# mLSTM's gate rows spread by DMA instead of by products, and HGRN2's first head with its filling products laid out anew

## What is computed

```
D[t, s] = exp(A_s - M_t) for s <= t, else 0
out_t   = sum_s D[t, s] (q_t . k_s) v_s / max(|sum_s D[t, s] (q_t . k_s)|, exp(-m_t))
```

## Time and profile before

| | |
|---|---|
| median of 3 runs | 1817.59 us (1816.62 to 1820.44) |
| the profiled execution | 1817.66 us, span 1815.8 us |
| mean granted clock of PE | 0.987 |
| PE | 1736.1 us busy, 96% |
| DVE, ACT, POOL | 1089.1 us (60%), 851.8 us (47%), 429.7 us (24%) |
| mLSTM | about 38 to 156 us of the span |
| HGRN2's first head | about 801 to 841 us |

### The profile page before, as it was taken

The page is one execution under the profiler, slowest core; times in us unless marked ns, Lnnn a source line. Parts: engine busy times, 40 slices in busy tenths (PEclk is TensorE's granted clock), DMA queues, the critical chain, the costliest instruction groups (busy, mean ns, idle before and its releaser), DMA issues. The chain is left out here.

```text
span 1815.8 us, 23867 instructions
## 1 busy us (share of the span) xinstructions
PE 1736.1 (96%) x8346; PEld 1396.6 (77%) x8346; DVE 1089.1 (60%) x1705; ACT 851.8 (47%) x1450; POOL 429.7 (24%) x332
## 2 busy tenths in 40 slices
PE   7998998999999999988999998999999989999997
PEld 5676887877888888777888887888888866677775
DVE  5545454458666643478878858765653377687343
ACT  5563555445333333456656645433332354255563
POOL 0332554110111100115554630111110013132232
PEclk9999999999999999999999999999999999999999
DMA  5111110231322232312112212222223222121121
GB/s 200 47 70 58 47 36 22 77 111 58 103 94 92 80 117 92 104 58 71 56 61 70 70 47 92 83 96 100 92 93 99 97 70 73 48 85 54 47 70 47
DMA packets 39904, 140.28 MB, mean 77 GB/s; under 512 B 4496, under 2 KB 4752, under 8 KB 39696
## 3 DMA queue, kind: packets, MB, share of 16 engines
q1 hardware_dynamic: 39824, 139.23, 22.6%
HBM read 137.11 MB, written 2.10 MB: 77 GB/s over the span
## 5 line engine op out<-in xcount | busy, mean ns | idle before, releaser
L187 PE MATMUL bank<-u_high,w_high 128*128 128x512 f32 x1580 | 649.8, 411 | 16.1 <-DVE m_on L1928 3.3
L189 PE MATMUL bank<-u_high,w_low 128*128 128x512 f32 x1580 | 621.0, 393 | 0.0
L188 PE MATMUL bank<-u_low,w_high 128*128 128x512 f32 x1580 | 620.7, 393 | 0.0
L187 PEld LDWEIGHTS bank<-u_high,w_high 128*128 128x128 f32 x1580 | 300.2, 190 | 102.5 <-issue 38.8
L189 PEld LDWEIGHTS bank<-u_high,w_low 128*128 128x128 f32 x1580 | 299.3, 189 | 65.8
L151 ACT ACTIVATE w_high<-w_ring 128x1024 fp32r<-128x1024 f32 x233 | 244.1, 1052 | 225.1 <-PE bank L189 173.1
L188 PEld LDWEIGHTS bank<-u_low,w_high 128*128 128x128 f32 x1580 | 300.5, 190 | 58.4 <-issue 3.8
L160 DVE TENSOR_TENSOR w_low<-w_ring,w_high 128x1024 fp32r<-128x1024 f32 x176 | 221.1, 1259 | 179.4 <-ACT w_high L151 179.2
L160 POOL TENSOR_TENSOR w_low<-w_ring,w_high 128x1024 fp32r<-128x1024 f32 x57 | 136.0, 2395 | 521.9 <-ACT w_high L151 521.8
L881 ACT ACTIVATE conv_up<-bank,col_sb 128x512 f32<-128x512 f32 x88 | 68.6, 780 | 270.5 <-DVE bank L936 270.5
L996 POOL TENSOR_TENSOR hidden<-conv_up 128x512 f32 x44 | 58.2, 1324 | 493.9 <-DVE conv_up L947 373.7
(11 more groups left out here) (413 smaller groups left out, 2316.5 us busy)
## 6 DMA issues: line engine op xcount, KB each, us to landing
w_ring<-ffn_up SPq DMA_DIRECT2D x88, 512.0 KB, 3.4
w_ring<-ffn_down SPq DMA_DIRECT2D x44, 512.0 KB, 3.4
w_ring<-c_in SPq DMA_DIRECT2D x32, 512.0 KB, 3.4
w_ring<-g_in SPq DMA_DIRECT2D x16, 512.0 KB, 4.2
w_ring<-m_in SPq DMA_DIRECT2D x12, 512.0 KB, 5.1
w_ring<-fox_in SPq DMA_DIRECT2D x12, 512.0 KB, 3.5
w_ring<-dsa_in SPq DMA_DIRECT2D x12, 512.0 KB, 3.5
w_ring<-ab_out SPq DMA_DIRECT2D x8, 512.0 KB, 4.4
```

Of the source, the lines that this page charges most:

```text
L187: nc.tensor.matmul(out, a[0], b[0], start=start, stop=False)
L188: nc.tensor.matmul(out, a[0], b[1], start=False, stop=False)
L189: return nc.tensor.matmul(out, a[1], b[0], start=False, stop=stop)
```

## The change

It has two parts.

In mLSTM: the eleven spreads by PE other than that of head 0's M are removed, with DVE's copies of them. In their place SP writes r_M, r_G and r_b (4 x 512 each, 8 KB) to a scratch in DRAM (`row_scratch`), waits for the writes to land, and reads them back with a source that repeats over the 128 partitions: M of heads 1 to 3 into a new tile `bcms`, G and b of four heads into `k.bcg`. These issues stand behind the loads of head 2's tiles and ahead of those of head 3's. DVE's arguments wait for `m_in`. PE's scores no longer wait for `spread_used`; those of head 1 wait for `cols_ready`, DVE's copy out of bank b4. The small columns are made at the end of DVE's head 1 instead of head 0, after a wait for `gb_in`; ACT's exponentials move from head 1 to head 2, DVE's last product from head 2 to head 3. PE's filling units are the same and keep their order; the two ahead of each spread join those that follow.

In HGRN2: the list for head 0 is [10, 12, 14, 16, 18, 20, 22, 24, 26, 27, 29, 32] instead of [16, 19, 20, 21, 22, 23, 24, 25, 26, 27, 28, 32], so ten units instead of sixteen stand ahead of the scores, and two instead of one behind each level. Head 1's f is projected into the output bank b_o instead of b_f, without the wait for head 0's f to be taken; the output of head 0 waits until DVE has taken it from there.

```diff
-    slots_first = [16, 19, 20, 21, 22, 23, 24, 25, 26, 27, 28, 32]
+    slots_first = [10, 12, 14, 16, 18, 20, 22, 24, 26, 27, 29, 32]
...
                     if m == 0:
                         k.wait_split(pe, 4 * h + s)
-                        pe.wait_ge((f_taken, q_taken, g_taken, v_ready)[s], h)
-                    ins = k.project(k.ps[s][:, :], s, None, m, m + 1)
+                        if h > 1 or s:
+                            pe.wait_ge((f_taken, q_taken, g_taken, v_ready)[s], h)
+                    ins = k.project((b_o if h == 1 and s == 0 else k.ps[s])[:, :], s, None, m, m + 1)
...
                 pe.wait_ge(at_done, 8 * h + 8)
+                if h == 0:
+                    pe.wait_ge(f_taken, 2)
...
-                nc.vector.tensor_tensor(out[:, :], k.ps[s][:, :], k.rn[:, :], ALU.mult).then_inc(done, 1)
+                bank = b_o if h == 1 and s == 0 else k.ps[s]
+                nc.vector.tensor_tensor(out[:, :], bank[:, :], k.rn[:, :], ALU.mult).then_inc(done, 1)
...
+    bcms = sb("m_M_next", [P, H - 1, T], F32)
+    rows = nc.dram_tensor("row_scratch", (3 * HA, T), F32).ap()
...
+            def spread_rows(out, kind, first, done):
+                n = HA - first
+                src = rows[kind * HA + first:(kind + 1) * HA, :].rearrange("(a h) t -> a h t", a=1).to_broadcast([P, n, T])
+                sp.dma_start(out, src).then_inc(done, 16)
+
             for h in range(2, H):
                 for s in range(3):
                     k.wait_split(sp, 3 * h - 3 + s)
                     k.load(sp, s, weights[3 * h + s, :, :])
+                if h == 2:
+                    sp.wait_ge(m_rows, 1)
+                    sp.dma_start(rows[0:HA, :], r_M).then_inc(rows_out, 16)
+                    sp.wait_ge(rows_out, 16)
+                    spread_rows(bcms[:, :, :], 0, 1, m_in)
+                    sp.wait_ge(g_rows, 1)
+                    sp.dma_start(rows[HA:2 * HA, :], r_G).then_inc(rows_out, 16)
+                    sp.wait_ge(b_ready, 1)
+                    sp.dma_start(rows[2 * HA:3 * HA, :], r_b).then_inc(rows_out, 16)
+                    sp.wait_ge(rows_out, 48)
+                    spread_rows(k.bcg[:, 0, :, :], 1, 0, gb_in)
+                    spread_rows(k.bcg[:, 1, :, :], 2, 0, gb_in)
...
                 pe.wait_ge(qk_ready, h + 1)
-                pe.wait_ge(bcm_ready, h + 1)
-                pe.wait_ge(spread_used, used[h])
+                if h == 0:
+                    pe.wait_ge(bcm_ready, 1)
+                if h == 1:
+                    pe.wait_ge(cols_ready, 1)
...
                 if n < H:
-                    pe.wait_ge(wt_ready, NT * h + NT)
-                    spread_row(b5, r_M, n).then_inc(m_spread, 1)
-                if n < H:
                     turn_v(n)
...
-                for i, (kind, g) in enumerate(spreads[h]):
-                    fill(2)
-                    if i == 0:
-                        pe.wait_ge(*((y_ready, h) if h else (cols_ready, 1)))
-                    elif i == 1:
-                        pe.wait_ge(bcm_ready, n + 1)
-                    else:
-                        pe.wait_ge(spread_used, used[h] + i - 1)
-                    spread_row(b_s[i % 2], (r_G, r_b)[kind], g).then_inc(spread, 1)
                 fill(len(units))
...
-                if h == 1:
+                if h == 2:
                     act.wait_ge(cols_done, 1)
...
-                dve.wait_ge(bcm_ready, h + 1)
+                dve.wait_ge(*((m_in, 16) if h else (bcm_ready, 1)))
+                m = bcms[:, h - 1, :] if h else bcm
...
-                for i, (kind, g) in enumerate(spreads[h]):
-                    dve.wait_ge(spread, used[h] + i + 1)
-                    nc.vector.tensor_copy(k.bcg[:, kind, g, :], b_s[i % 2][:, :]).then_inc(spread_used, 1)
-                if h == 0:
-                    dve.wait_ge(spread_used, H)
+                if h == 1:
+                    dve.wait_ge(gb_in, 32)
+                    dve.wait_ge(cols_ready, 1)
...
-                if h == 2:
+                if h == 3:
                     dve.wait_ge(cols_exp, 1)
```

More of the change, by code:

```diff
@@ L1510, in mlstm @@
     acc, vraw, on, bcm = (sb(f"m_{s}", [P, T], F32) for s in "acc v_raw on M".split())
+    bcms = sb("m_M_next", [P, H - 1, T], F32)
+    rows = nc.dram_tensor("row_scratch", (3 * HA, T), F32).ap()
+    (rows_out, m_in, gb_in) = (sem("row_" + s) for s in ("out", "m_in", "gb_in"))
     q, kk = (sb(f"m_{s}", [DK, T], F32) for s in "q k".split())
@@ L1522, in mlstm @@
     gb = lambda i: k.p("gbias", i)[0:HA]
-    (raw_taken, if_ready, tanh_done, f_soft, ab_taken, a_soft, b_ready, m_rows, g_rows, m_turned, m_cols, e_ready, g_turned, spread, spread_used,
+    (raw_taken, if_ready, tanh_done, f_soft, ab_taken, a_soft, b_ready, m_rows, g_rows, m_turned, m_cols, e_ready, g_turned,
      cols_ready, cols_exp, cols_done) = (sem("ab_" + s) for s in (
-         "raw_taken if_ready tanh_done f_soft ab_taken a_soft b_ready m_rows g_rows m_turned m_cols e_ready g_turned spread spread_used "
+         "raw_taken if_ready tanh_done f_soft ab_taken a_soft b_ready m_rows g_rows m_turned m_cols e_ready g_turned "
          "cols_ready cols_exp cols_done").split())
@@ L1530, in mlstm @@
          "d_masked st_done wt_ready num_done den_taken squared tot_ready on_scaled o_turned y_ready ch_act ch_dve ch_pool").split())
-    spreads = {0: [(0, h) for h in range(H)], 1: [(1, 0), (1, 1)], 2: [(1, 2), (1, 3)], 3: []}
-    used = {h: sum(len(spreads[g]) for g in range(h)) for h in range(H + 1)}
     def cs(c):
@@ L1904, in body @@
                 if n < H:
-                    take_m(n)
                     arguments(n)
@@ L1950, in _ @@
             dve.wait_ge(m_cols, 1)
-            take_m(0)
+            take_m()
             arguments(0)
```

8 lines of the change are left out of this document (4 added, 4 removed).

## The result

The changed kernel takes 1799.21 us, the median of 4 runs (1799.07 to 1801.34), against 1817.52 (1816.62 to 1820.44, 4 runs) for the kernel before beside it: a ratio of 0.9899, 95% interval 0.9882 to 0.9916, or 18.3 us. The forecast was 1797.6 with a range of 1794.0 to 1803.0.

What follows compares the result with a forecast made beforehand. PE was taken as the bound, busy 1736.1 of 1815.8 us. From 1817.66 us, 15.8 for mLSTM and 4.3 for HGRN2's first head were subtracted, giving 1797.6 us, with a range of 1794.0 to 1803.0.

Steps and rivals of the forecast that it cites:

- M spreads: mLSTM heads 1 to 3: removing three row spreads of M from PE saves 1.06 us each, 3.2 us.
- joint to head 3: mLSTM, end of head 2: last b spread and the 0.99 us wait for VectorE's copy go, 2.10 us.
- 1.7 us for the clock: mLSTM, after the gap before head 3's scores: work lost to the low clock, counted as won.
- The broadcasts: mLSTM, SP's queue: at some 400 GB/s M lands near 53, G and b near 64, cost 0.
- B: Rival: broadcasts slow at 82 GB/s, PE stands for head 3's tile, 7 us given back, 1804.6; chance 0.08.
- C: Rival: broadcasts delay head 3's loads over 20 us, PE stands after head 1's scores; one case 1819.6; chance 0.05.
- HGRN2's first head: HGRN2 head 0: earlier start and scores, fewer waits and steady clock win 4.4 us, taken as 4.3.
- VectorE's earlier work may slow GpSimd: HGRN2 head 0: GpSimd's factor pairs may lengthen beside VectorE's earlier work; 0.1 us taken off.
- moves with it: HGRN2 head 0: the chain to the turned keys follows level 4's merge, 3.4 us earlier, 834.07 becoming 830.65.
- 33.0 us is work: HGRN2 head 0, PE's start to head 1's scores: 39.5 us less 4.8 of waits and 1.7 of clock.
- The bank: HGRN2 head 0's start: projecting into the output bank lets PE start at 801.15 instead of 801.94, 0.8 us.
- A of the rivals: HGRN2's first head or head 3's joint: clock falls again, or waits return; 1799.3 to 1801.0; chance 0.17.

Runs made afterwards that it cites:

- m_one_engine: Changed kernel with M's broadcast issued in two parts, to 127 partitions and to the last one: 1806.89 us (one run).
- only_mlstm: Changed kernel with its three HGRN2 edits undone, leaving the mLSTM part alone: 1797.9 us, ratio 0.9903 to the kernel before.
- bank_only: Changed kernel with HGRN2's old list of products for head 0, keeping the new bank: 1799.33 us, ratio 0.9904 to the kernel before.
- late_queries: Changed kernel; HGRN2 head 0: split of head 1's fourth tile earlier, list ending 26, 28, 30, 32, GpSimd's decayed queries after all factors: 1799.33 us.
- pool_order: Changed kernel, with GpSimd making the factors of levels 4 and 5 before decayed keys and queries in HGRN2's head 0: 1800.73 us (one run).

## Why the prediction was right, and where it was not

- **mLSTM, 15.8 us forecast, 16.2 measured.** The price of a spread of G or b, 1.26 us with its joints, was 1.24. The M spreads, priced at 1.06, were worth 1.2 to 1.3, which is most of why it came to more than forecast. The joint to head 3 was priced at 2.10 us and gave 1.9 when it was put back alone. The 1.7 us for the clock came as 1.5 to 1.6 in the profiled executions. The reason I gave, the gap "and two slow spreads", fits the four traces that bear on it, since either without the other lowered nothing, but it is not proven. Head 1's scores were forecast near 82.8 and head 3's near 122; they stood at 81.89 and 121.43, and 0.6 of that is the earlier opening.
- **The broadcasts, forecast at no cost, cost none.** Landing near 53 and 64 was forecast; M landed at 53.3, G and b near 62 and 65. B and C of the rivals fell for this shape. `m_one_engine` shows that C's place was the right one, and that it would have had a considerable price for M alone: 11.2 us.
- **Moved filling products** met no wait at all, as forecast; neither did the column work, moved one head later.
- **HGRN2's first head, 4.3 us forecast, 2.28 measured.** The step that failed is "VectorE's earlier work may slow GpSimd", for which the prediction took 0.1 us off, with its companion, that the chain of the turned keys "moves with it", 3.4 us earlier. Counted from PE's start, level 0 came at 11.06 us against 10.98 forecast, so up to there the sum holds, though PE waited 0.7 us of it and not 1.3. Level 4 came at 21.94 against 21.16: up to its factor GpSimd's chain was 0.7 us longer (1.5 in all). The turned keys came at 31.17 against 29.5: they moved 1.8 us against the stage's start, not 3.4, since level 4 and with it its merge came 0.8 to 0.9 later than forecast and VectorE's two key steps took 1.73 us from start to end instead of 0.99. Another 0.5 went behind them, most of it the unforeseen wait of 0.82 us for the state. Waits sum to 3.9 us (0.39, 0.29, 1.51, 0.91, 0.82), not 2.9. That is 1.0 of the 2.1 missing; the other 1.1 is that all the rest of the head took 34.1 us and not the "33.0 us is work" of the prediction. About 0.3 of it is the low clock, which had cost this head 1.4 us rather than 1.7 (from the chunk states to the filling products behind the output, before and after, less the wait and one product); the remainder I can only put down to pauses too short to carry a bracket, as ahead of the scores at 789.76.
- **The bank, forecast 0.8 us.** A start that is 0.8 us earlier on an engine which the others pace is worth nothing: 38.95 us against 38.93.
- **A of the rivals, the clock.** No fall of the clock in head 0 nor at head 3's joint; its waits did come back, 1 us more than forecast. The clock took part elsewhere: 1.7 us won between the stages, 2.0 lost from 1520 on, and my carried sum had neither. That these two nearly cancel is luck.

The sum by steps: 0.6 (opening) + 16.2 + 1.7 + 2.3 - 0.3 - 2.0 = 18.5 us of span, against 20.1 forecast. The 1.6 us between are HGRN2's first head (2.0), its other heads (0.3) and the work outside the change (2.0 - 1.7 = 0.3), less mLSTM's 0.4 and the opening's 0.6.

## What to carry to other kernels

Where PE is the bound, a small product that only copies a row to all partitions can be priced from the distance between two of them, and a DMA broadcast from a scratch can replace it at no cost if it is wanted tens of us later and all 128 partitions lead its pattern. Where PE waits in a head that VectorE and GpSimd both work for, add up their instructions at the durations that they have beside each other, not alone, before expecting a better order of PE's products to help; and ask of every earlier start which engine paces the stretch.

## What the runs showed of the hardware that was not expected

- A broadcast of 768 KB from three rows in DRAM to 128 partitions landed 3.7 us after its issue, two of 1 MB issued one behind the other 4.7 and 6.8 after theirs. On one DMA engine 762 KB of it ran at 26 GB/s, and the issue alone held SP's queue for 12.5 us, so that everything behind it was late, the 8 KB writes included.
- The sharing between VectorE and GpSimd moves time and doesn't save it: a 128x256 product of GpSimd took 0.72 to 1.87 us, its 128x512 product of the decayed keys 1.28 to 2.36, and VectorE's two-operand steps on 128x512 0.69 to 1.77, depending on what the other engine was in, while GpSimd's whole chain kept to 16.7 to 17.0 us in all the orders tried with the new list (15.4 with the old one).
- The granted clock falls in the same few places of unchanged code, but not in every execution and not for the same length. Between mLSTM and HGRN2 that made 645.0 to 647.0 us of the same work, from the scores of HGRN2's last head to the end 771.7 to 777.2. It is as large as HGRN2's whole gain or larger, so that gain can be read in the trace and not in the time.
- At one place of head 0, behind PE's wait for the turned keys, the clock fell where that wait was 3.5 or 2.0 us (3.5 in the kernel before, `only_mlstm` and `bank_only`, 2.0 in `late_queries`) and stayed up where it was 1.4 or less (the changed kernel 0.91, `pool_order` 1.4).
